# Norms of the query and key blocks: sums of squares as two fp32r products, one unit later

## The chip, the cores and the metric

One core of one Trainium2 chip runs the whole program. The metric is device time of one execution in microseconds; three runs of the kernel before took 979.59, 981.25 and 982.6 us. The profile is of a separate execution.

## The reference

The program is one decoder layer for 1040 prompt rows (16 learned meta tokens and 1024 tokens) and 8 sample rows. Only this part matters here:

```python
z = h @ w_in                                   # 1048 x 3592
qkv, new_buf_qkv = _causal_dwconv(qkv_raw, buf_qkv, conv_qkv_w)   # width 4
qkv = jax.nn.silu(qkv)
q, k, v = jnp.split(qkv, 3, axis=-1)
q = _l2norm(q.reshape(b, length, 4, 128)) * (128 ** -0.5)   # x * rsqrt(sum(x*x) + EPS)
k = _l2norm(k.reshape(b, length, 4, 128))
# then a chunked gated delta rule on q, k, v, an output projection,
# and a mixture of 32 experts of which each row takes 2
```

So each query and key head, a block of 128 channels, is divided by the root of its sum of squares, row by row. In the kernel channels are partitions and rows are columns, so the sum over channels is a sum over partitions. TensorE makes it, as a product of a 128 x 128 matrix of ones with the squares.

## The kernel before, in words

All engines run programs of their own, in a fixed order written out by hand; semaphores hold one back for another. The first half of the program, called the front here, is organised by **units**. The projection has 28 blocks of 128 channels (`NBLK`); each block is made in three units, one for each third of the rows (350 columns), and `UNITS` lists all 84 in order. One unit is 24 matmuls at L1157: eight slices of the inner dimension by three products of high and low parts in fp32r, a format that TensorE multiplies faster than plain fp32 and with fewer bits. `ENDS` gives, for a unit k, the block whose last third it is. Blocks 0 and 1 are interleaved: block 0 ends with unit 3, block 1 with unit 5, block 2 with unit 8, and from there each block n ends with unit 3n+2. Blocks 0 to 7 are keys and queries in turn (`QK` = 8; even ones keys), blocks 8 to 11 values, 12 to 15 gates, 16 to 27 the other mixer.

Every engine has a loop over k, and in step k it does what the order puts there. ScalarE's step k starts when unit k's product is complete, since it copies that third out of PSUM. For a query or key block n that ends with unit e the steps before the change are:

- step e, ScalarE: the last third to `raw`, the first tap of the convolution to `acc` (L672), a strip to `hist`, then `high(n+2)`, the high part `wh` of the weights of block n+2 (L633). VectorE: `weight_low(n+2)`, the low part `wl` (L859), then `conv(n)`, three more taps (L901).
- step e+1: tanh on ScalarE into `th` (L780), `silu(n)` on VectorE (L908) into `acc`.
- step e+2: Square of `acc` into `th` on ScalarE (L788).
- step e+3: TensorE, `square_sums(n)` (L1180) after unit e+3: three plain fp32 products of 358 columns into banks 3 to 5. A plain fp32 product appears as two records, so a group is six. ScalarE: Ln (L765) and Exp (L768, L770), the root's reciprocal, into `th`. Each needs another activation table, so two ACT_TABLE_LOADs belong to it.
- step e+4: VectorE, `normalized(n)` (L913), the product of `acc` and `th`. It gives `kn_ok`.
- step e+5: SyncE writes `acc` to DRAM (L552); ScalarE copies the sample columns (L795).

Around these stand the steps for the decay and key matrices of head h. In step 10+6h TensorE makes `key_products(h)` (L1195) after unit 10+6h, which wait for the normalized block 2h and for Ln of block 2h+1. VectorE copies one block of them (`last_keys`) and makes `decay_args(h)` (L925, L927) when the rows `ar` are loaded. In step 11+6h ScalarE takes their exponential (L774), in step 12+6h VectorE makes `lower(h)` (L935 to L940). SyncE, in order: in step 13+6h it stores both (L538, L540); in step 14+6h it waits until the second store has landed (L542) and loads pieces of it as `lp` (L545); in step 15+6h, which is step 9 of the next head, it loads `ar` and `br` of head h+1 (L533, L499). Block weights are loaded in step e (L494).

Two more places are touched. In step 6 VectorE makes `al` and four small tiles `src` from the decay (L1093 to L1099); in step 7 TensorE transposes `src` after unit 7 (L1307). And from step 35 on VectorE makes an elimination in 38 steps (`eliminate`, L959 and L961) that the chunk stage, from unit 51, needs.

Of the kernel before, what the change touches and what calls it, by code (L numbers as in the profile page):

```python
# [5 lines left out]
F32 = mybir.dt.float32  # L6
F32R = mybir.dt.float32r
I32 = mybir.dt.int32
U32 = mybir.dt.uint32
ALU = mybir.AluOpType  # L10
ACT = mybir.ActivationFunctionType
AX = mybir.AxisListType

P = 128
# [7 lines left out]
TILES = 9  # L22
# [4 lines left out]
QK = 2 * H  # L27
QKV = 3 * H
# [53 lines left out]
def later(i):  # L82
# [9 lines left out]
         ("row_act", 27), ("hi_ok", 18), ("wh_ok", 28), ("wab_hi", 1), ("raw_ok", 12), ("tap0_ok", 12),  # L92
         ("ab_copied", 1), ("th_ok", 12), ("col_a", 9), ("sq_ok", 8), ("rk_act", 16), ("rows_copied", 1),
         ("decay_ok", 4), ("xt_ok", 1), ("kd_ok", 9), ("vc_ok", 9), ("uc_ok", 9), ("o_act", 27), ("normed", 9),
         ("lo_ok", 18), ("wl_ok", 28), ("wab_lo", 1), ("scaled", 3), ("conv_ok", 12), ("col_v", 13),
         ("sl_ok", 12), ("kn_ok", 8), ("kk8_ok", 4), ("diff_ok", 4), ("arg_ok", 4), ("at1_ok", 4), ("at2_ok", 4),
# [140 lines left out]
HALF = 358  # L237
# [4 lines left out]
ENDS = {UNITS.index((n, 2)): n for n in range(NBLK)}  # L242


def end_of(n):

    return UNITS.index((n, 2))
# [62 lines left out]
def front_parts(nc, m, s, b, io):  # L310

    ps = b.psum
# [16 lines left out]
    for k in range(3):  # L329
        at = m.at  # L330
# [7 lines left out]
    th = [m.place(f"th{k}", [P, RLEN]) for k in two]  # L338
# [45 lines left out]
    ck, dt, at, er, nb = [], [], [], [], []  # L384
    for p in two:
        if p == 1:
# [14 lines left out]
    hb = [m.place(f"hb{k}", [P, D]) for k in two]  # L401
    junk = m.place("junk", [P, D])
    wbc = m.place("wbc", [P, D])
    wab = m.place("wab", [P, KD, 8])
    wab1 = m.place("wab1", [P, KD, 16], F32R)
    wab2 = m.place("wab2", [P, KD, 16], F32R)
# [5 lines left out]
    turned, hi_ok, lo_ok, wab_hi, wab_lo = s("turned"), s("hi_ok"), s("lo_ok"), s("wab_hi"), s("wab_lo")  # L412
    w_landed, wh_ok, wl_ok = s.pair("w_landed", 3), s("wh_ok"), s("wl_ok")
    z_done, z_free = s("z_done"), s.pair("z_free", 3)
    ab_ok, ab_copied, ab_turned, zeroed, scaled = (s("ab_ok"), s("ab_copied"), s("ab_turned"), s("zeroed"),
                                                   s("scaled"))
    col_v, col_a, cum_ok, rows_ok, rows_copied, rows_out, zero_out = (
        s("col_v"), s("col_a"), s("cum_ok"), s("rows_ok"), s("rows_copied"), s("rows_out"), s("zero_out"))
    raw_ok, kept, tap0_ok, taps, conv_ok, th_ok, sl_ok = (s("raw_ok"), s("kept"), s("tap0_ok"), s("taps"),
                                                          s("conv_ok"), s("th_ok"), s("sl_ok"))  # L420
    sq_ok, ss_ok, kn_ok, smp_ok = s("sq_ok"), s("ss_ok"), s("kn_ok"), s("smp_ok")
# [45 lines left out]
    def sync(sp):  # L467
# [53 lines left out]
        for k in range(len(UNITS)):  # L521
            n = ENDS.get(k)
# [18 lines left out]
            if 0 <= h < H and ph == 5:  # L541
                sp.wait_ge(at_out, 16 * (h + 1))  # L542
                for blk in range(NS):
                    p0, lo = (blk * H + h) * NC, SB * blk
                    sp.dma_start(lp[p0:p0 + NC, :, :], at_d[:, lo:lo + SB, h, lo:lo + SB]).then_inc(lp_in, 16)  # L545
            for n in (ENDS.get(k - 5), ENDS.get(k - 2)):
                if n is not None and n == ENDS.get(k - 5 if n < QK else k - 2) and n < QKV:
                    if n < QK:
                        sp.wait_ge(kn_ok, n + 1)
                    else:  # L550
                        sp.wait_ge(sl_ok, n + 1)
                    sp.dma_start(qkv_d[conv_index(n), :, 0:PROMPT], acc[n % 3][:, 0:PROMPT]  # L552
                                 ).then_inc(qkv_out[n % 3], 16)
            n = ENDS.get(k - 3)
# [36 lines left out]
            if 0 <= p - 1 < NC and ph == 1:  # L591
                c = p - 1
# [32 lines left out]
    def scalar(act):  # L625
# [103 lines left out]
        for k in range(2, len(UNITS)):  # L729
# [27 lines left out]
            if k == 8:  # L757
                act.wait_ge(rows_ok, 1)
                a_(rows_t[:, :, :], ps[0:2 * NC * H, 7, 0:256].rearrange("p (q t) -> p q t", q=2)[:, :, 0:CH],
                   ACT.Copy).then_inc(rows_copied, 1)  # L760
            n = ENDS.get(k - 3)
            if n is not None and n < QK:
                act.wait_ge(ss_ok, n + 1)
                rk = th[n % 2][:, 0:3 * HALF]
# [21 lines left out]
            if n is not None and n < QK:  # L786
                act.wait_ge(sl_ok, n + 1)
                a_(th[n % 2][:, 0:QLEN], acc[n % 3][:, 0:QLEN], ACT.Square).then_inc(sq_ok, 1)  # L788
            n = ENDS.get(k - 5)
            if n is not None and n < QKV:  # L790
                if n < QK:
                    act.wait_ge(kn_ok, n + 1)
                else:
                    act.wait_ge(sl_ok, n + 1)
                a_(b.smp[:, conv_index(n), :], every(acc[n % 3], QS, KQ), ACT.Copy).then_inc(smp_ok, 1)  # L795
# [42 lines left out]
    def vector(dve):  # L838
# [71 lines left out]
        def normalized(n):  # L910
            dve.wait_ge(sl_ok, n + 1)
            dve.wait_ge(rk_ok.sem, rk_ok.at(n + 1))
            tt(acc[n % 3][:, 0:QLEN], acc[n % 3][:, 0:QLEN], th[n % 2][:, 0:QLEN], ALU.mult).then_inc(kn_ok, 1)  # L913

        def last_keys(h):
            dve.wait_ge(kk_ok, h + 1)
            if h >= 1:
                dve.wait_ge(at1_ok, h)
            V.tensor_copy(kk8[:, :], ps[0:CH, 5, 380:380 + CH]).then_inc(kk8_ok, 1)
# [30 lines left out]
        def identity():  # L950
            inv_step(V.memset(xi[:, :, :], 0.0))
            inv_step(V.memset(xi[:, :, :].rearrange("p r j -> p (r j)")[:, 0:SB * SB:SB + 1], 1.0))
# [71 lines left out]
        for k in range(len(UNITS)):  # L1024
# [6 lines left out]
                softplus_decay()  # L1031
            if k == INV0:
                identity()
            n = ENDS.get(k)
            if n is not None and n + 2 < NBLK and n not in ahead:
                weight_low(n + 2)
# [66 lines left out]
                conv(n)  # L1103
            if n is not None and n >= QKV + H and (n - QKV - H) % 3 == 1:
                conv_a((n - QKV - H) // 3)
            n = ENDS.get(k - 4)
            if n is not None and n < QK:
                normalized(n)
            n = ENDS.get(k - 1)
# [19 lines left out]
    def tensor(pe):  # L1129
# [40 lines left out]
            ins.then_inc(ab_ok, 1)  # L1170

        def square_sums(n):
            pe.wait_ge(sq_ok, n + 1)
            pe.wait_ge(ab_copied, 1)
            if n >= 1:
                pe.wait_ge(ln_ok.sem, ln_ok.at(n))
            if n >= 2:
                pe.wait_ge(kk8_ok, n // 2)
            for c in range(3):
                ins = mm(ps[:, 3 + c, 0:HALF], b.ones[:, :], th[n % 2][:, HALF * c:HALF * c + HALF],  # L1180
                         start=True, stop=True)
            ins.then_inc(ss_ok, 1)

        def key_products(h):
# [105 lines left out]
        for k in range(4, len(UNITS)):  # L1290
            unit(k)
            if k == 4:
                pe.wait_ge(ab_copied, 1)
                pe.wait_ge(scaled, 1)
                for t in range(10):
                    lo, n = (t * CH, length(t)) if t < NC else (PROMPT, SAMPLES)
                    ins = tp(ps[0:n, 6, 16 * t:16 * t + 16], ab[:, lo:lo + n], b.ident[0:16, 0:16])
                ins.then_inc(ab_turned, 1)
            if k == 6:
                pe.wait_ge(col_v, G_STEP)  # L1300
                mm(ps[0:CH, 6, 160:196], b.upto[0:CH, 0:CH], g[0:CH, 0:NC, :], start=True, stop=True)
                mm(ps[0:SAMPLES, 6, 196:200], b.ident[0:SAMPLES, 0:SAMPLES], g[0:SAMPLES, NC, :], start=True, stop=True)
                mm(ps[:, 6, 200:236], b.ones[0:CH, :], g[0:CH, 0:NC, :], start=True, stop=True).then_inc(cum_ok, 1)
            if k == 7:
                pe.wait_ge(col_v, SRC_STEP)
                for q in two:
                    ins = tp(ps[0:2 * NC * H, 7, 128 * q:128 * q + CH],  # L1307
                             src[0:CH, 2 * q:2 * q + 2, :, :].rearrange("p k c h -> p (k c h)"), b.ident[0:CH, 0:CH])
                ins.then_inc(rows_ok, 1)
            n = ENDS.get(k - 3)  # L1310
            if n is not None and n < QK:
                square_sums(n)
            h, ph = (k - 10) // 6, (k - 10) % 6
            if 0 <= h < H and ph == 0:
                key_products(h)
            p, ph = phase(k)
            if 0 <= p - 1 < NC:
                (chain_0, chain_1, chain_2)[ph](p - 1)
            if 0 <= p < NC:
                (prepare_0, prepare_1, prepare_2)[ph](p)  # L1320
            if 0 <= p - 2 < NC and (ph == 2 if p - 2 < NC - 1 else ph == 1):
                output(p - 2)
# [1753 lines left out]
```

## Time and profile before

| | |
|---|---|
| median of 3 runs | 981.25 us |
| profiled execution, whole time | 979.38 us |
| its span | 977.6 us |
| granted TensorE clock, mean | 0.994 |
| TensorE matmul busy | 946.4 us, 97% |
| VectorE busy | 698.6 us, 71% |
| ScalarE busy | 491.2 us, 50% |
| GpSimd busy | 191.5 us, 20% |

The span runs from the first to the last recorded instruction; 1.8 us of the profiled execution lie outside it. Busy shares are averages over stages of different kinds. In the timelines of the profile, the first number is the start in us from the start of the span, the second the time covered by the piece, and "x6" the number of records in it. A bracket at the end gives the time for which the engine was idle just before, and what released it. Matmul records overlap: each lasts about 0.32 us in a unit, while the next starts after 0.16.

### The profile page before, as it was taken

The page shows a single profiled execution, that of the slowest core. Times are in us where ns is not written, and L with a number is a line of the kernel's source. Part 1 is how long each engine was busy: PE and PEld are TensorE (multiplying, and loading weights), DVE is VectorE, ACT ScalarE, POOL GpSimd, SP SyncE. Part 2 cuts the span into 40 slices and gives each one's busy share as a digit, 9 for nine tenths or more (in the row PEclk, how much of TensorE's full clock was granted, in tenths as well). Part 3 has the DMA queues.
Part 4 walks back from the last instruction along what each step waited for, and adds up shares of the span by engine and source line. Part 5 has one row for each costly group of instructions (what it writes and reads, how often), then busy time and mean ns, then how long its engine had stood idle before and what let it go on. Part 6 is the DMA issues. An engine that isn't in the chain of part 4 may idle for free.

```text
span 977.6 us, 14810 instructions
## 1 busy us (share of the span) xinstructions
PE 946.4 (97%) x5408; PEld 817.8 (84%) x5408; DVE 698.6 (71%) x1059; ACT 491.2 (50%) x890; POOL 191.5 (20%) x153
## 2 busy tenths in 40 slices
PE   5999999999899999999999998999999999999996
PEld 4889999999899999999888885667777777777762
DVE  7466677789453634546666666769999999999996
ACT  7578778432423222232422313246666666666794
POOL 2000000000000000000030001315555555554414
PEclk9999999999999999999999999999999999999999
DMA  7104775623755664446833235999999999999994
GB/s 253 52 22 136 176 160 134 176 88 128 229 135 151 166 165 116 123 145 185 290 103 124 71 112 199 345 407 415 412 415 409 409 400 415 396 413 411 393 396 161
DMA packets 123499, 230.61 MB, mean 236 GB/s; under 512 B 71528, under 2 KB 84386, under 8 KB 114734
## 3 DMA queue, kind: packets, MB, share of 16 engines
q1 hardware_dynamic: 108102, 202.69, 60.0%
q0 software_dynamic: 15264, 26.92, 7.4%
q8 instruction: 37, 0.61, 0.3%
q14 instruction: 24, 0.20, 0.1%
q10 hardware_dynamic: 72, 0.20, 0.1%
HBM read 205.33 MB, written 53.11 MB: 264 GB/s over the span
## 4 chain that ended last, share of the span: by engine, by line
PE 86%; DVE 8%; ACT 3%; DMA 1%; issue 1%; SPq 0%; POOL 0%; POOLq 0%; ACTq 0%; DVEq 0%
PE psum L1157 26%; PE psum L2421 12%; PE psum L2075 10%; PE psum L2511 8%; PE psum L2425 5%; PE psum L2357 3%; PE psum L2405 3%; DVE xi L961 2%; DVE it L959 2%; PE psum L2478 2%; PE psum L1180 2%; PE psum L2010 1%; PE psum L1262 1%; DVE acc L901 1%; PE psum L1249 1%
## 5 line engine op out<-in xcount | busy, mean ns | idle before, releaser
L1157 PE MATMUL psum<-hh,wh 128*128 128x350 f32 x672 | 222.7, 331 | 0.7 <-ACT acc L690 0.7
L1157 PE MATMUL psum<-hh,wl 128*128 128x350 f32 x672 | 217.2, 323 | 0.0
L1157 PE MATMUL psum<-hl,wh 128*128 128x350 f32 x672 | 216.5, 322 | 0.0
L1157 PEld LDWEIGHTS psum<-hh,wh 128*128 128x128 f32 x672 | 127.1, 189 | 2.2 <-ACT acc L690 1.0
L1157 PEld LDWEIGHTS psum<-hl,wh 128*128 128x128 f32 x672 | 126.9, 189 | 0.9
L1157 PEld LDWEIGHTS psum<-hh,wl 128*128 128x128 f32 x672 | 126.6, 188 | 0.0
L2395 DVE TENSOR_TENSOR wgu_lo<-wgu,wgu_hi 128x1536 fp32r<-128x1536 f32 x60 | 105.4, 1758 | 17.1 <-ACT wgu_hi L2390 17.0
L2390 ACT ACTIVATE wgu_hi<-wgu 128x1536 fp32r<-128x1536 f32 x60 | 89.3, 1489 | 2.1 <-DMA new_ssm_sample<-s_in 2.1
L2421 PE MATMUL psum<-wgu_hi,xgt_hi 128*128 128x512 f32 x180 | 85.6, 475 | 0.0
L1702 POOL IOTA r_iw<- 128x8 f32 x1 | 0.1, 144 | 410.5 <-DMA mixer_rows<-th 410.5
L859 DVE TENSOR_TENSOR wl<-wst,wh 128x1024 fp32r<-128x1024 f32 x28 | 34.3, 1225 | 58.8 <-ACT wh L633 58.7
L2349 POOL DMA_INDIRECT sum_rows<-total,slot_rows x32 | 66.5, 2078 | 23.5 <-issue 22.1
L2421 PE MATMUL psum<-wgu_lo,xgt_hi 128*128 128x512 f32 x180 | 70.8, 393 | 0.0
L2421 PE MATMUL psum<-wgu_hi,xgt_lo 128*128 128x512 f32 x180 | 70.7, 393 | 0.0
L2491 DVE TENSOR_TENSOR wd_lo<-wd,wd_hi 128x2048 fp32r<-128x2048 f32 x30 | 68.8, 2292 | 1.2
L2118 POOL DMA_INDIRECT xg<-h_rows,slot_rows x34 | 63.5, 1869 | 24.3 <-DVE slot_rows L1933 10.3
L2343 POOL DMA_INDIRECT before<-sum_rows,slot_rows x34 | 34.4, 1012 | 149.2 <-DVE total L2524 142.9
L2487 ACT ACTIVATE wd_hi<-wd 128x2048 fp32r<-128x2048 f32 x30 | 57.7, 1923 | 0.0
L2425 PE MATMUL psum<-wgu,xgt_rest 128*128 128x512 f32 x120 | 56.3, 591 | 0.0
L2375 ACT ACTIVATE xgt_hi<-psum 128x768 fp32r<-128x768 f32 x30 | 24.4, 813 | 61.6 <-PE psum L2357 61.6
L901 DVE SCALAR_TENSOR_TENSOR acc<-raw,cqw,acc 128x1072 f32<-128x1072 f32 x36 | 48.0, 1334 | 0.9
L2075 PE MATMUL psum<-wo_hi,yt_hi 128*128 128x512 f32 (+1 forms) x144 | 47.8, 413 | 0.0
(376 smaller groups left out, 1887.5 us busy)
## 6 DMA issues: line engine op xcount, KB each, us to landing
wgu<-w_gate SPq DMA_DIRECT2D x34, 1024.0 KB
wgu<-w_up SPq DMA_DIRECT2D x34, 1024.0 KB
wd<-w_down SPq DMA_DIRECT2D x34, 1024.0 KB, 13.6
wst<-w_in SPq DMA_DIRECT2D x28, 512.0 KB, 4.2
ck<-qkv_rows SPq DMA_DIRECT2D x9, 702.0 KB
qkv_rows<-acc SPq DMA_DIRECT2D x12, 520.0 KB, 6.4
xb<-x SPq DMA_DIRECT2D x8, 512.0 KB, 4.3
wo<-w_out SPq DMA_DIRECT2D x8, 512.0 KB, 7.1
```

Of the source, the lines that this page charges most:

```text
L901: stt(ac[:, 0:QLEN], rw[:, q:q + QLEN], w[:, q:q + 1], ac[:, 0:QLEN], ALU.mult, ALU.add).then_inc(taps if q < KQ - 1 else conv_ok, 1)
L1157: ins = mm(ps[:, c, 0:ZC], w[:, kk, :], a[:, kk, c * ZC:(c + 1) * ZC], start=(kk == 0 and q == 0), stop=(kk == KD - 1 and q == 2))
L2075: ins = mm(ps[0:n, 2 * (t % 2) + c, :], y, w[:, c * 512:c * 512 + 512], start=(i == 0 and q == 0), stop=(i == KD - 1 and q == 2))
L2118: pool.indirect_dma_start(b.xg[k][:, :], None, b.h2_dram, bass.IndirectOffsetOnAxis(ap=b.slot_rows[:, e:e + 1].bitcast(U32), axis=0), boun ...
L2349: pool.indirect_dma_start(b.sum_d, rows_of(e), rows[:, :], None, bounds_check=TOK - 1, oob_is_err=False).then_inc(q.sum_out.sem, 16)
L2390: nc.scalar.activation(w_hi[x.p][h][:, :, :, :], half_of(b.slots[x.k][0], h), ACT.Copy).then_inc(w_hi_ok[h][x.p].sem, 1)
L2395: nc.vector.tensor_tensor(half_of(b.slots[x.k][1], h), half_of(b.slots[x.k][0], h), w_hi[x.p][h][:, :, :, :].bitcast(F32), ALU.subtract).t ...
L2421: ins = nc.tensor.matmul(gate_up_bank(x.p), a[:, kk, :], w, start=(kk == 0 and i == 0), stop=(kk == KP - 1 and i == 2))
L2425: nc.tensor.matmul(gate_up_bank(x.p), xt_rest[x.p][:, kk - KP, :], raw[:, :, kk, :], start=False, stop=False)
L2487: nc.scalar.activation(wd_hi[x.p][:, :, :], b.slots[x.k][2][:, :, :], ACT.Copy).then_inc(wd_hi_ok[x.p].sem, 1)
L2491: nc.vector.tensor_tensor(b.slots[x.k][3][:, :, :], b.slots[x.k][2][:, :, :], wd_hi[x.p][:, :, :].bitcast(F32), ALU.subtract).then_inc(wd_ ...
L2511: ins = nc.tensor.matmul(ps[0:C, 4 + 2 * x.p + c, :], h[x.p][:, f, :], w[:, f, c * 512:c * 512 + 512], start=(f == 0 and i == 0), stop=(f ...
```

## The change

The squares are split in two as the weights are: ScalarE rounds `th` to fp32r in a new tile `sq_hi`, VectorE subtracts it and gives `sq_lo`. TensorE then makes six fp32r products in place of three plain ones. Everything behind Square moves by one step: sums, Ln and Exp from e+3 to e+4, `normalized` from e+4 to e+5, the store to DRAM and the copy of sample columns from e+5 to e+6. `square_low` stands ahead of `weight_low` in VectorE's step e+3. Both new tiles have one buffer, so the rounding of block n waits for the sums of block n-1 (`ss_ok`). They lie where the input rows lay in the normalization before the front, so the first waits for that too.

```diff
+    sq_hi = m.place("sq_hi", [P, 3 * HALF], F32R, at=pool_b)
+    sq_lo = m.place("sq_lo", [P, 3 * HALF], F32R, at=pool_b + 4320)
...
 # SyncE
-            for n in (ENDS.get(k - 5), ENDS.get(k - 2)):
-                if n is not None and n == ENDS.get(k - 5 if n < QK else k - 2) and n < QKV:
+            for n in (ENDS.get(k - 6), ENDS.get(k - 2)):
+                if n is not None and n == ENDS.get(k - 6 if n < QK else k - 2) and n < QKV:
...
 # ScalarE
-            n = ENDS.get(k - 3)
+            n = ENDS.get(k - 4)
             if n is not None and n < QK:
                 act.wait_ge(ss_ok, n + 1)
...
                 a_(th[n % 2][:, 0:QLEN], acc[n % 3][:, 0:QLEN], ACT.Square).then_inc(sq_ok, 1)
-            n = ENDS.get(k - 5)
-            if n is not None and n < QKV:
+                act.wait_ge(sq_ok, 3 * n + 1)
+                if n == 0:
+                    act.wait_ge(lo_ok, 2 * TILES)
+                else:
+                    act.wait_ge(ss_ok, n)
+                a_(sq_hi[:, :], th[n % 2][:, 0:3 * HALF], ACT.Copy).then_inc(sq_ok, 1)
+            n = ENDS.get(k - 6) if ENDS.get(k - 6, QK) < QK else ENDS.get(k - 5)
+            if n is not None and n < QKV and (n >= QK or k == end_of(n) + 6):
...
 # VectorE
+        def square_low(n):
+            dve.wait_ge(sq_ok, 3 * n + 2)
+            if n >= 1:
+                dve.wait_ge(ss_ok, n)
+            tt(sq_lo[:, :], th[n % 2][:, 0:3 * HALF], sq_hi[:, :].bitcast(F32), ALU.subtract).then_inc(sq_ok, 1)
...
+            n = ENDS.get(k - 3)
+            if n is not None and n < QK:
+                square_low(n)
             n = ENDS.get(k)
             if n is not None and n + 2 < NBLK and n not in ahead:
                 weight_low(n + 2)
...
-            n = ENDS.get(k - 4)
+            n = ENDS.get(k - 5)
             if n is not None and n < QK:
                 normalized(n)
...
 # TensorE
         def square_sums(n):
-            pe.wait_ge(sq_ok, n + 1)
+            pe.wait_ge(sq_ok, 3 * n + 3)
...
             for c in range(3):
-                ins = mm(ps[:, 3 + c, 0:HALF], b.ones[:, :], th[n % 2][:, HALF * c:HALF * c + HALF],
-                         start=True, stop=True)
+                for q, part in enumerate((sq_hi, sq_lo)):
+                    ins = mm(ps[:, 3 + c, 0:HALF], b.ones[:, :].bitcast(F32R), part[:, HALF * c:HALF * c + HALF],
+                             start=(q == 0), stop=(q == 1))
...
-            n = ENDS.get(k - 3)
+            n = ENDS.get(k - 4)
             if n is not None and n < QK:
                 square_sums(n)
```

## Rows read from the trace of the kernel before

**Rows 1.** The page's chain that ended last: share of the span by engine.

```profile
PE 86%; DVE 8%; ACT 3%; DMA 1%; issue 1%; SPq 0%; POOL 0%; POOLq 0%; ACTq 0%; DVEq 0%
```

**Rows 2.** The chain in order of time: start us, us, engine, tile and line.

```profile
68.67 3.87 PE psum L1157 x24
...
82.03 1.84 PE psum L1195 x18
...
87.74 1.81 PE psum L1180 x6
...
169.55 26.94 PE psum L1157 x168
```

**Rows 3.** Busy time of each engine in one stretch of two blocks (us, busy, count).

```profile
101.09:129.66 28.57, 28.57 (x176) 27.23 (x175) 20.53 (x20) 22.47 (x31) 0.00 (x0) 1.00 0.63 153
```

**Rows 4.** Timeline of PE: steps 6 and 7, and the later wait at L1204.

```profile
62.30 2.08 PE L1180 MATMUL psum<-th,ones 128*128 128x358 f32 x6 [1.09 <-ACT th L788]
...
68.28 0.40 PE L1307 MATMUL psum<-ident,src 117*72 117x117 f32 x2
...
261.01 1.08 PE L1204 MATMUL psum<-inv_d,at 117*117 117x117 f32 x8 [2.00 <-DMA inv_t<-inverse_columns]
```

**Rows 5.** Timeline of DVE, steps 5 to 9.

```profile
63.15 4.08 DVE L901 SCALAR_TENSOR_TENSOR acc<-raw,cqw,acc 128x1072 f32<-128x1072 f32 x3
...
68.03 0.20 DVE L1099 SCALAR_TENSOR_TENSOR src<-beta_col,e_col 128x36 f32<-128x36 f32 x1
...
75.53 1.23 DVE L859 TENSOR_TENSOR wl<-wst,wh 128x1024 fp32r<-128x1024 f32 x1 [4.01 <-ACT wh L633]
76.68 4.07 DVE L901 SCALAR_TENSOR_TENSOR acc<-raw,cqw,acc 128x1072 f32<-128x1072 f32 x3
80.84 1.28 DVE L913 TENSOR_TENSOR acc<-acc,th 128x1072 f32<-128x1072 f32 x1
```

**Rows 6.** Timeline of ACT, steps 6 to 8.

```profile
64.41 1.16 ACT L765 ACTIVATE th<-psum,eps 128x1074 f32<-128x1074 f32 x1 [0.24 <-PE psum L1180]
65.58 1.28 ACT L768 ACT_TABLE_LOAD   x1
66.88 1.10 ACT L768 ACTIVATE th<-th 128x1074 f32<-128x1074 f32 x1
...
72.57 0.45 ACT L658 ACTIVATE raw<-psum 128x340 f32<-128x340 f32 x1 [1.10 <-PE psum L1157]
...
74.46 1.04 ACT L633 ACTIVATE wh<-wst 128x1024 fp32r<-128x1024 f32 x1
```

**Rows 7.** Timeline of SP's queue, steps 13 to 15, and of DVE, step 16.

```profile
101.91 0.32 SPq L540 DMA_DIRECT2D lower_blocks<-at_a  x1
...
107.53 1.37 SPq L545 DMA_DIRECT2D lp<-lower_blocks  x3
108.94 0.39 SPq L533 DMA_DIRECT2D ar<-scale_rows  x1
...
114.86 1.26 DVE L925 TENSOR_TENSOR dt_a<-ar,cum 117x1053 f32<-117x1053 f32 x1 [2.12 <-DMA ar<-scale_rows]
```

**Rows 8.** Tile ar: issue to landing of its four loads.

```profile
DMA to landing us min/median/max: 5.2/5.8/6.1
```

**Rows 9.** Tile br: issue to landing of its four loads.

```profile
DMA to landing us min/median/max: 6.4/7.1/8.6
```

**Rows 10.** Timeline of PE near 610 us.

```profile
604.38 2.90 PE L1518 MATMUL psum<-ident,uu 128*128 128x128 f32 x24
608.83 0.41 PE L2018 MATMUL psum<-r_os,before 128*128 128x32 f32 x2 [1.55 <-DVE r_os L1871]
...
610.81 0.66 PE L2027 MATMUL psum<-r_spread,r_in_slot 128*128 128x64 f32 x4 [1.35 <-DVE r_in_slot L1892]
611.31 5.42 PE L1518 MATMUL psum<-ident,uu 128*128 128x128 f32 x32
```

**Rows 11.** One microsecond of that stretch; the granted clock is third from last.

```profile
612.00:613.00 1.00, 1.00 (x7) 1.00 (x6) 0.01 (x1) 0.00 (x0) 0.09 (x1) 0.50 1.07 451
```

More of the change, by code:

```diff
@@ L92 @@
          ("row_act", 27), ("hi_ok", 18), ("wh_ok", 28), ("wab_hi", 1), ("raw_ok", 12), ("tap0_ok", 12),
-         ("ab_copied", 1), ("th_ok", 12), ("col_a", 9), ("sq_ok", 8), ("rk_act", 16), ("rows_copied", 1),
+         ("ab_copied", 1), ("th_ok", 12), ("col_a", 9), ("sq_ok", 24), ("rk_act", 16), ("rows_copied", 1),
          ("decay_ok", 4), ("xt_ok", 1), ("kd_ok", 9), ("vc_ok", 9), ("uc_ok", 9), ("o_act", 27), ("normed", 9),
```

## The prediction

> **What bounds the kernel now.** I read the chain by engine first: TensorE has 86% of it, VectorE 8% [rows 1]. Then the chain in order of time: from unit 6 to unit 35 it never leaves TensorE, whose units, square sums and key products follow each other without a gap until 196.5 us, where the long piece that starts at 169.55 ends [rows 2]. A unit costs 3.87, a group of square sums 1.81 with the switch to plain fp32 and back, a group of key products 1.84 [rows 2]. From 196.5 us VectorE's elimination sets the pace up to the chunk stage; it starts behind unit 35 in program order, so what is won or lost up to there reaches the end one to one. Two blocks with one group of key products take 28.57 us, in which ScalarE is busy 22.47 and VectorE 20.53 [rows 3]: neither bounds a steady pair, but both are full enough for a moved step to count. The one gap of TensorE near the change is 1.09 us ahead of the first group [rows 4].
>
> **The product.** A matmul of 350 columns costs 3.87 / 24 = 0.161 us in a unit [rows 2]; with 358 columns I take 0.163, so six cost 0.98. The group before costs 1.81. Saved: 0.83 per group, 6.6 over eight. The bounds of the new group are 0.97 (six matmuls of a unit) and 1.81 (bits of the switch kept, nothing won).
>
> **The added work beside it.** The rounding of 1074 columns on ScalarE: 1.04 for 1024 columns [rows 6], so about 1.1. VectorE's subtraction: 1.23 for 1024 [rows 5], of which the next instruction overlaps some 0.1; I take 1.2. Per pair ScalarE comes to 22.47 + 2.2 = 24.7 and VectorE to 20.53 + 2.5 = 23.0, against a shortened 28.57 - 1.66 = 26.9. Throughput holds. What must be followed is the order, at three places.
>
> **Place 1, step 7.** TensorE's transposes of `src` start at 68.28, as the last `src` tile is made (68.03 + 0.20) [rows 4, 5]: they were just not late, because the first group filled TensorE's time. Now that group stands in step 7 behind the transposes, so unit 7 follows directly on step 6's small products, at about 61.2, and ends at 65.2. Meanwhile `square_low(0)` stands in VectorE's step 6 behind three taps (end 67.2) [rows 5] and ahead of `al` and `src`: `src` is ready 1.2 later, at 69.4. TensorE stands idle for 4.2 us. Then transposes 0.39, first group 0.98, and unit 8 begins at 70.85 where it began at 68.67: +2.2, with the 1.09 gap and the 2.08 group of before already set against it.
>
> **Place 2, step 10.** The first key products need `normalized(0)`. It stood in step 7; block 0 ends with unit 3, so it now stands in step 8, behind `conv(2)` on VectorE. The chain, from durations less their overlap: first group done 70.9; Ln 1.18, table 1.30, Exp 1.01 [rows 6]; Square 1.1 and rounding of block 1 1.05; ScalarE is free at 76.5, where unit 8 ends at 74.7. Its step 8 takes from 72.57 to the end of `wh`, 75.4, some 2.9 to 3.0 [rows 6], so `wh` is ready at 79.5. Then `weight_low` 1.15, three taps 4.0, product 1.27 [rows 5]: 86.0. TensorE is there at 74.7 + 3.87 + 0.98 + 3.87 = 83.4 and waits 2.6. Key products 1.84 and unit 11 end at 91.8; before, they ended at 87.74 [rows 2]: +4.0.
>
> **The clock.** After gaps of 1.55 and 1.35 us close together the granted clock was 0.50, that is 1.2 GHz, at 612 [rows 10, 11], and 32 matmuls took 5.42 where 24 had taken 2.90 (0.121 each, so 3.87 for 32): 1.55 dearer [rows 10]. After a single gap of 2.00 us at 261.01, eight matmuls took 1.08, with no sign of that [rows 4]. The 4.2 us of place 1 are longer than either, so I count one fall there. It doubles transposes and first group, 1.1 us, which lies on the chain of place 2; the rest, in unit 8, is covered by ScalarE, free 1.8 later than that unit ends. The 2.6 of place 2 shrinks to about 2.1, like the one without a fall. So +1.1, bounds 0 and 3.1 (a second fall, at place 2, with the 1.55 and some of it uncovered). The Trainium skill, "TensorE: Matmul & The Clock Gate", section "What's actually happening", says that the throttled clock is the default and that activity releases it. By that rule the gap of place 1 is paid for again at 1.2 GHz. The rows at 612 agree.
>
> At the end of unit 11 the new kernel is 4.0 + 1.1 = 5.1 behind.
>
> **From there to the last group.** Six groups save 6 x 0.83 = 5.0. Two couplings take some of it back.
> - *VectorE in step e+5.* In odd blocks `lower` ends about 14.2 after unit e's end (store issued at 101.91, unit 11 ended at 87.74) [rows 2, 7]; now `normalized` (1.2) and the next `square_low` (1.2) follow: 16.6. TensorE wants the low part at 3 x 3.85 + 0.98 + 3.85 = 16.4. Blocks 3, 5 and 7: 0.2 each, 0.5 in all (0 to 1.5).
> - *Place 3, SyncE's queue.* The store of `acc` moves from step 13, ahead of the wait for the lower blocks to land, to step 14, behind it and behind `lp`, ahead of `ar` and `br` of the next head. From the end of unit 14: the lower blocks are issued at 1.7 (before 0.8, since the period is shorter); they land 4.5 later (5.6 before, with two transfers behind, now one; bounds 3.5 and 5.6); `lp` 1.4 [rows 7], the store 0.5; `ar` is issued at 8.1. It now has a 520 KB transfer right ahead, as `br` had: `br` lands after 6.4 to 8.6, median 7.1, `ar` after 5.2 to 6.1 [rows 8, 9]. So it lands at 15.2. `decay_args` 2.56 and the low part 1.2 make 19.0, and TensorE wants that at 0.25 + 14.4 + 3.85 = 18.5. Before, VectorE waited 2.12 for `ar` at 114.86 [rows 7] with no one behind it in a hurry; now `square_low` of blocks 4 and 6 is queued there. 0.5 each, 1.0 in all; bounds 0 (landing at 6.4) and 6 (both at 8.6 and slow stores).
>
> **Sum.** 5.1 - 5.0 + 0.5 + 1.0 = +1.6 us at the end of unit 28, carried through to the end. The memory of the new tiles and the one step less of room in `th` cost nothing: tanh of block n+2 comes well behind `normalized(n)` in the steady part, and in step 9 it waits where place 2 already stands. The late copy of sample columns is 0.2 us on ScalarE as before. Against the profiled execution: 979.38 + 1.6 = 981.0. This execution lies 1.9 below the median 981.25, so for the median I say 981.25 + 1.6, about 982.9.
>
> **Rivals.**
> 1. *The arithmetic alone*: the reordering costs nothing. 6.6 from the groups and 1.4 from the first one's gap (1.09) and dearer record (2.08 against 1.81): -8.0, 973. For it: TensorE is the chain throughout. Against it: VectorE's and ScalarE's steps 6 to 8 are in program order, and `src` is already just in time. With only half of places 1 and 2 it would be -4 to -6. 0.15.
> 2. *The loop through SyncE decides*: lower blocks, landing, `lp`, store, `ar`, `decay_args`, `square_low`, square sums. If `ar` lands over 7.6 us after issue, each further microsecond holds TensorE in two heads, and ScalarE's exponential behind it. At `br`'s slowest landing, with stores of 5.6, it is 3 per head in place of 0.5: +1.6 + 5.0 = +6.6; half of that +4, and this with or without a second fall of the clock. 985 to 988. For it: the transfers of a pair come in one burst and the slack of before is 2.1. Against: `ar` never took over 6.1. 0.25.
> 3. *fp32r with the matrix of ones bitcast runs no faster than plain fp32*: six products of the old 0.6, so 8 x (3.6 - 1.8) = 14 slower. The units at 0.161 speak against it. 0.05.
>
> **How the numbers follow.** My case has 0.55, with its own range -1.0 (no fall of the clock, no coupling: 4.0 - 5.0) to +4. A measurement of this kernel can tell about 0.3%, 2.9 us, from no change. Slower than that: 0.25 and 0.05 of the rivals; the tail of my own case beyond +2.9 is about what rival 2 gives back below it. Faster: 0.15. Same: 0.55. The range of 8 in 10 leaves out rivals 1 and 3: 977 to 987.5.
>
> **What would show it.** In the changed kernel: L1307 starts at about 69.5 with some 4 us idle ahead of it, released by VectorE; matmuls behind it at about twice 0.161 for a few microseconds; L1195 near 86 to 87 with about 2 idle, released by VectorE's product; the six records of the sums covering 1.0 us; unit 11 ending at 91.8 to 92.9; later short waits of the sums for `sq_lo`, the longest behind `ar`; the last key products ending 1 to 2 us later than 169.55. I am wrong if TensorE shows no gap at step 7 or 10 (rival 1), if waits of over 1.5 us stand ahead of the sums of blocks 4 and 6 (rival 2), or if the end of unit 35 and the end of the kernel move by different amounts.

## The result, and the profile after

The changed kernel took 983.95 us in the median of 21 runs, against 981.25 us before; the ratio is 1.0026, 95% interval 1.0015 to 1.0037, so 1.5 to 3.6 us slower. 982.9 was forecast, with a range of 977 to 987.5. The profiled execution took 983.95 us, with a span of 982.1, which is 4.5 us more than that of before; the median moved by 2.7.

The one place to read the change at is the end of unit 35, ahead of the elimination. Executions start with transfers, and what follows them starts up to 1.6 us earlier or later, so I count from the small products of step 6 (`upto`, in both kernels the same work up to there), which start at 60.44 before and 60.65 after. ScalarE's copy of the last third of unit 35, which starts when the unit's product is complete, in ScalarE's timeline before and then after:

```profile
196.51 0.46 ACT L658 ACTIVATE raw<-psum 128x340 f32<-128x340 f32 x1 [1.68 <-PE psum L1157]
...
198.91 0.46 ACT L660 ACTIVATE raw<-psum 128x340 f32<-128x340 f32 x1 [1.68 <-PE psum L1174]
```

That is 136.07 and 138.26 us behind the mark: +2.19. Place 1 in TensorE's timeline after, to be held against [rows 4]; L1174 is the unit, L1198 the sums, L1325 the transposes:

```profile
65.03 0.32 PE L1174 MATMUL psum<-hh,wl 128*128 128x350 f32 x1
69.66 0.61 PE L1325 MATMUL psum<-ident,src 117*72 117x117 f32 x2 [4.30 <-DVE src L1116]
69.94 0.65 PE L1198 MATMUL psum<-sq_hi,ones 128*128 128x358 f32 x1
70.38 0.50 PE L1198 MATMUL psum<-sq_lo,ones 128*128 128x358 f32 x1
70.67 0.50 PE L1198 MATMUL psum<-sq_hi,ones 128*128 128x358 f32 x1
70.97 0.50 PE L1198 MATMUL psum<-sq_lo,ones 128*128 128x358 f32 x1
...
71.87 0.49 PE L1174 MATMUL psum<-hh,wh 128*128 128x350 f32 x1
...
73.08 0.33 PE L1174 MATMUL psum<-hh,wl 128*128 128x350 f32 x1
73.25 0.33 PE L1174 MATMUL psum<-hh,wh 128*128 128x350 f32 x1
```

The bracket shows a gap of 4.30 us and who ended it. From sum to sum it is 0.30 us, against 0.17 from 73.08 to 73.25: that is the low clock. Busy times in the stretch itself (the granted clock, third from last, is 0.50, that is 1.2 GHz):

```profile
69.60:72.70 3.10, 3.04 (x11) 3.03 (x12) 1.28 (x2) 1.32 (x2) 0.00 (x0) 0.50 0.03 5
```

VectorE after, to be held against [rows 5]. The low part L927 sits between the taps and `src`; at 85.78 is `normalized(0)`, behind the taps of block 2:

```profile
63.36 4.08 DVE L909 SCALAR_TENSOR_TENSOR acc<-raw,cqw,acc 128x1072 f32<-128x1072 f32 x3
67.35 1.27 DVE L927 TENSOR_TENSOR sq_lo<-th,sq_hi 128x1074 fp32r<-128x1074 f32 x1
...
69.41 0.20 DVE L1116 SCALAR_TENSOR_TENSOR src<-beta_col,e_col 128x36 f32<-128x36 f32 x1
...
81.79 4.07 DVE L909 SCALAR_TENSOR_TENSOR acc<-raw,cqw,acc 128x1072 f32<-128x1072 f32 x3
85.78 1.27 DVE L921 TENSOR_TENSOR acc<-acc,th 128x1072 f32<-128x1072 f32 x1
```

Place 2, and then the groups of blocks 3 and 4, in TensorE's timeline after:

```profile
87.10 2.10 PE L1213 MATMUL psum<-acc 128*117 128x117 f32 x18 [2.11 <-DVE acc L921]
...
109.74 0.43 PE L1198 MATMUL psum<-sq_hi,ones 128*128 128x358 f32 x1 [0.32 <-DVE sq_lo L927]
110.01 0.33 PE L1198 MATMUL psum<-sq_lo,ones 128*128 128x358 f32 x1
110.17 0.32 PE L1198 MATMUL psum<-sq_hi,ones 128*128 128x358 f32 x1
...
124.93 0.43 PE L1198 MATMUL psum<-sq_hi,ones 128*128 128x358 f32 x1 [0.55 <-DVE sq_lo L927]
```

From the last matmul of a unit to the first of the next, less the 0.16 that it takes anyway, a group before costs 1.53, and the switch back to fp32r 0.28 more behind it: the 1.81 of [rows 2]. After, the groups of blocks 2 to 7 cost 0.99, 1.57, 1.80, 1.01, 1.19 and 1.35. 0.99 is the bare product; the other 1.97 us are waits for the low part. Such a wait costs some 0.25 more than the idle time in its bracket (0.58 for the 0.32 of block 3): 0.16 because that idle time is counted from the end of a record, while the next one otherwise starts 0.16 ahead of it, and the rest because the first step behind it is longer (109.74 to 110.01 is 0.27, the next step 0.16). For block 4 the wait comes through SyncE's queue and VectorE, to be held against [rows 7, 8]:

```profile
107.33 0.32 SPq L542 DMA_DIRECT2D lower_blocks<-at_a  x1
...
112.58 1.15 SPq L547 DMA_DIRECT2D lp<-lower_blocks  x3
113.77 0.38 SPq L554 DMA_DIRECT2D qkv_rows<-acc  x1
114.20 1.53 SPq L535 DMA_DIRECT2D ar<-scale_rows  x1
```

```profile
121.14 1.26 DVE L939 TENSOR_TENSOR dt_a<-ar,cum 117x1053 f32<-117x1053 f32 x1 [2.15 <-DMA ar<-scale_rows]
122.43 1.26 DVE L941 TENSOR_TENSOR dt_a<-dt_a,negmask 117x1053 f32<-117x1053 f32 x1
123.61 1.27 DVE L927 TENSOR_TENSOR sq_lo<-th,sq_hi 128x1074 fp32r<-128x1074 f32 x1
```

The account: unit 11 ends 5.13 us later than before, the six groups win 6 x 1.81 - 7.91 = 2.95, which leaves 2.18. The page's chain of the execution after looks quite different from [rows 1]:

```profile
PE 74%; DVE 9%; DMA 7%; ACT 4%; issue 3%; POOL 1%; SPq 1%; POOLq 0%; ACTq 0%; DVEq 0%
```

Some 113 us have left TensorE in it. Cut into stretches, the chain is on TensorE for 134 of the 150 us from 50 to 200 before and for 66 after: at each small wait it goes over to VectorE, ScalarE or a transfer and stays there for a while, so these shares say little of what a wait costs. Another 30 us left between 600 and 650 us and 14 behind 930, in stages that the change does not touch. Nor do these stages take the same time in each execution: from the experts' product L2425 (L2443 after) at 650.20 and 652.25 to the first record of TensorE's last product, L2305 (L2323 after), it is 316.7 us before and 318.9 after, and in the experiments 317.7 to 321.4, in no order of the change. These 2.2 us are the other half of the 4.5 between the two spans. So the spans of single executions are not compared below, only the end of unit 35 and the ratios of many runs.

### The profile page after: what moved, and what is told of

It is laid out like the page before. It is cut to its first block, busy times and chain, and to the rows that moved or that the text cites. A ratio compares the mean times of both kernels' runs of the same rounds, so it can differ in the third digit from the quotient of the medians.

```text
span 982.1 us, 14840 instructions
## 1 busy us (share of the span) xinstructions
PE 944.6 (96%) x5408; PEld 820.0 (83%) x5408; DVE 707.0 (72%) x1067; ACT 499.2 (51%) x898; POOL 191.2 (19%) x153
## 4 chain that ended last, share of the span: by engine, by line
PE 74%; DVE 9%; DMA 7%; ACT 4%; issue 3%; POOL 1%; SPq 1%; POOLq 0%; ACTq 0%; DVEq 0%
PE psum L1174 20%; PE psum L2439 13%; PE psum L2093 11%; PE psum L2529 8%; PE psum L2443 5%; PE psum L2375 3%; DMA new_ssm_sample<-s_in 2%; DVE xi L975 2%; DVE it L973 2%; DVE acc L909 1%; PE psum L2028 1%; DMA y<-sum_rows 1%; DVE wl L867 1%; PE psum L1280 1%; PE psum L1267 1%
## 5 line engine op out<-in xcount | busy, mean ns | idle before, releaser
L1174 PE MATMUL psum<-hh,wh 128*128 128x350 f32 x672 | 220.9, 329 | 0.7 <-ACT acc L692 0.7
L1174 PE MATMUL psum<-hh,wl 128*128 128x350 f32 x672 | 217.5, 324 | 0.0
L1174 PE MATMUL psum<-hl,wh 128*128 128x350 f32 x672 | 216.7, 322 | 0.0
L1174 PEld LDWEIGHTS psum<-hh,wh 128*128 128x128 f32 x672 | 127.4, 190 | 1.3 <-ACT acc L692 0.9
L1174 PEld LDWEIGHTS psum<-hl,wh 128*128 128x128 f32 x672 | 127.1, 189 | 0.0
L1174 PEld LDWEIGHTS psum<-hh,wl 128*128 128x128 f32 x672 | 126.8, 189 | 0.0
L2443 PE MATMUL psum<-wgu,xgt_rest 128*128 128x512 f32 x120 | 56.3, 591 | 0.0
```

Source lines behind the costliest of these rows:

```text
L1174: ins = mm(ps[:, c, 0:ZC], w[:, kk, :], a[:, kk, c * ZC:(c + 1) * ZC], start=(kk == 0 and q == 0), stop=(kk == KD - 1 and q == 2))
L2443: nc.tensor.matmul(gate_up_bank(x.p), xt_rest[x.p][:, kk - KP, :], raw[:, :, kk, :], start=False, stop=False)
```

## The experiments

Each was executed twelve times, e8 six times. Ratios are to the kernel before, executed beside them; most intervals are 2 to 4 us to either side, so for steps of a microsecond the end of unit 35, counted from step 6's small products, decides.

| kernel | ratio, 95% interval | end of unit 35, us | against before |
|---|---|---|---|
| before | 1 | 136.07 | |
| changed | 1.0026, 1.0015 to 1.0037 | 138.26 | +2.19 |
| e1 product alone | 0.9967, 0.9939 to 0.9996 | 131.83 | -4.24 |
| e2 order alone | 1.0059, 1.0034 to 1.0083 | 142.64 | +6.57 |
| e3 filled gap | 1.0043, 1.0000 to 1.0086 | 137.05 | +0.98 |
| e4 first norm | 1.0012, 0.9974 to 1.0050 | 135.95 | -0.12 |
| e5 src first | 1.0014, 0.9995 to 1.0034 | 138.16 | +2.09 |
| e6 store back | 1.0013, 0.9983 to 1.0043 | 138.57 | +2.50 |
| e7 first two old | 0.9976, 0.9952 to 0.9999 | 133.10 | -2.97 |
| e8 high only | 0.9923, 0.9894 to 0.9953 | 129.74 | -6.33 |
| e9 early ar | 1.0010, 0.9986 to 1.0033 | 138.06 | +1.99 |
| e10 both | 0.9971, 0.9945 to 0.9996 | 132.79 | -3.28 |
| e11 low before norm | 0.9944, 0.9911 to 0.9978 | 131.10 | -4.97 |

### The product and the order apart

```diff
 # e1, on the kernel before
-                a_(th[n % 2][:, 0:QLEN], acc[n % 3][:, 0:QLEN], ACT.Square).then_inc(sq_ok, 1)
+                a_(sq_hi[:, 0:QLEN], acc[n % 3][:, 0:QLEN], ACT.Square).then_inc(sq_ok, 1)
...
+                for q in range(2):
+                    ins = mm(ps[:, 3 + c, 0:HALF], b.ones[:, :].bitcast(F32R), sq_hi[:, HALF * c:HALF * c + HALF],
+                             start=True, stop=True)
```

> The order of the kernel before, every step where it was; Square writes its result straight into an fp32r tile, and each of the three products is made twice from it as fp32r, so that TensorE has the six matmuls of the change and nothing else is added. Left out: the low part of the squares. Theory (the product saves 0.83 us a group, the moved order takes it back at the start): 8 x 0.83 and the 1.4 us at the first group, 8.0 us faster than before; of that 1.09 may stay, since the first group still waits for Square: 6.9 to 8.0 faster, about 974. Rival (the product itself saves little in place, since ScalarE and VectorE set the pace of a pair of blocks): within 2 us of before.

Measured: 3.2 us faster by the ratio, 4.24 at unit 35; neither the 7 to 8 of the theory nor the rival's 2 at most. Four of its groups cost 0.98 and three 1.44; those three wait for Square:

```profile
100.91 1.25 PE L1187 MATMUL psum<-sq_hi,ones 128*128 128x358 f32 x6 [0.19 <-ACT sq_hi L794]
```

Its first group still waits for Square and then the transposes for `src` (0.8). So in the old place the sums are bound to ScalarE as soon as a pair of blocks gets shorter, and the gain of the product alone is about half of 8.0. The move by one unit does answer something.

```diff
 # e2, on the changed kernel
-                for q, part in enumerate((sq_hi, sq_lo)):
-                    ins = mm(ps[:, 3 + c, 0:HALF], b.ones[:, :].bitcast(F32R), part[:, HALF * c:HALF * c + HALF],
-                             start=(q == 0), stop=(q == 1))
+                ins = mm(ps[:, 3 + c, 0:HALF], b.ones[:, :], th[n % 2][:, HALF * c:HALF * c + HALF],
+                         start=True, stop=True)
```

> The changed kernel with its order, its rounding and its subtraction, but the three plain fp32 products of th as before. Theory: it has the gaps of steps 7 and 10, the fall of the clock, and a first group dearer by some 1.2 us at the low clock; after unit 11 no gain and no loss: 6 to 7 us slower than before, 4 us slower than the changed kernel. Rival (the added work costs wherever it stands, some 0.6 us a pair of blocks, and the start only 1 or 2): 3 to 4 us slower than before, spread evenly over blocks 0 to 7.

Measured: +5.8 us by the ratio, +6.57 at unit 35, near the theory's 6 to 7. Its two gaps are 4.31 and 1.67, its groups from block 2 on cost 1.53 or 1.54 each, without a wait, and a pair of blocks takes 28.55 as before: all of the loss lies ahead of unit 11. The rival, a price spread evenly, is out.

### The start: clock, first product, src

```diff
 # e3, on the changed kernel
             if k == 7:
+                for q in range(24):
+                    mm(ps[:, 7, 0:ZC], wh[0][:, q % KD, :], hh[:, q % KD, 0:ZC], start=True, stop=True)
                 pe.wait_ge(col_v, SRC_STEP)
```

> The changed kernel with 24 extra fp32r matmuls of 350 columns behind unit 7, ahead of the wait for src, into a bank that is written anew right after: 3.9 us of work in the 4.3 us gap. Theory (the gap lets the clock fall to 1.2 GHz, and what this costs the first group and the transposes lies on the chain to the key products): the matmuls behind the gap are at 0.16 us from start to start, unit 11 ends 1.1 us earlier than in the changed kernel, and the whole is 1.1 faster than that, +1.4 against before. Rival (the slow matmuls are hidden by the wait of step 10 anyway): no change against the changed kernel, +2.5 against before.

The extra matmuls are L1324; the gap shrinks to 0.48, and the same stretch as above runs at full clock:

```profile
70.83 0.39 PE L1327 MATMUL psum<-ident,src 117*72 117x117 f32 x2 [0.48 <-DVE src L1116]
70.98 0.41 PE L1198 MATMUL psum<-sq_hi,ones 128*128 128x358 f32 x1
71.24 0.33 PE L1198 MATMUL psum<-sq_lo,ones 128*128 128x358 f32 x1
71.40 0.33 PE L1198 MATMUL psum<-sq_hi,ones 128*128 128x358 f32 x1
```

```profile
69.60:72.70 3.10, 2.62 (x17) 2.33 (x16) 2.31 (x7) 2.32 (x5) 0.00 (x0) 1.00 0.00 0
```

The unit behind the first key products starts 27.32 behind the mark, against 28.32 in the changed kernel: 1.00 of the forecast 1.1. Unit 35 ends 1.21 earlier. In the ratio, whose interval is 8 us wide (1.0000 to 1.0086), that can't be seen.

```diff
 # e4, on the changed kernel
-            n = ENDS.get(k - 5)
-            if n is not None and n < QK:
+            n = 0 if k == 7 else ENDS.get(k - 5)
+            if n is not None and n < QK and (n > 0 or k == 7):
                 normalized(n)
```

> The changed kernel with normalized(0) in VectorE's step 7 instead of step 8, ahead of the three taps of block 2. Theory (the first key products wait for it alone): the 2.1 us gap ahead of them is gone, and the whole is 2.1 faster than the changed kernel, +0.4 against before, within 0.4. Rival (Ln of block 1, or the rows that ScalarE copies in step 8, come as late): a gap of 1 to 2 us stays ahead of the key products with another releaser, and less than 1 us is won.

TensorE goes on without a gap, where the changed kernel waits 2.11:

```profile
85.21 0.32 PE L1174 MATMUL psum<-hh,wl 128*128 128x350 f32 x1
85.37 0.88 PE L1213 MATMUL psum<-acc 128*117 128x117 f32 x7
```

Unit 35 ends 2.31 earlier than in the changed kernel, 0.12 earlier than before. One instruction of VectorE, one step earlier, takes the whole loss of the change back at unit 35; the ratio, 0.9974 to 1.0050, can't tell it from either kernel.

```diff
 # e5, on the changed kernel: square_low(0) no longer ahead of weight_low in step 6, but here
                 assert cols == SRC_STEP
+                square_low(0)
```

> The changed kernel with square_low(0) behind the src tiles in VectorE's step 6 instead of ahead of them. Theory (what TensorE stands for in step 7 is VectorE's order, taps first, and both the transposes and the first group hang on it): the gap ahead of the transposes shrinks by 1.2 us to 3.1, but the first group now waits some 0.5 for the low part, so it starts only 0.3 to 0.5 earlier; unit 35 ends 0.3 to 0.6 earlier than in the changed kernel. Rival (the transposes alone hold it): 1.2 us earlier.

```profile
69.20 0.39 PE L1326 MATMUL psum<-ident,src 117*72 117x117 f32 x2 [3.13 <-DVE src L1116]
```

3.13 of gap as expected, then 0.92 for the low part, where some 0.5 was expected: the unit behind the key products starts 0.47 earlier (27.85 against 28.32), as the theory said. But only 0.10 is left at unit 35, since the group of block 4 costs 2.13 instead of 1.80. What is won ahead is taken by that wait: first sign that the later waits are a chain of their own.

### The later waits

```diff
 # e6, on the changed kernel
-            for n in (ENDS.get(k - 6), ENDS.get(k - 2)):
-                if n is not None and n == ENDS.get(k - 6 if n < QK else k - 2) and n < QKV:
+            for n in (ENDS.get(k - 5), ENDS.get(k - 2)):
+                if n is not None and n == ENDS.get(k - 5 if n < QK else k - 2) and n < QKV:
```

> The changed kernel with SyncE's store of a query or key block back in step e+5, ahead of lp, ar and br. Theory (the groups of blocks 4 and 6 wait for ar through decay_args and the low part): ar is issued about when it is now but lands about 1 us sooner, as before; TensorE's interval at the group of block 4 falls from 1.80 to 1.0 to 1.2 us, that of block 3 (1.57, which hangs on lower) stays; unit 35 ends 0.6 to 1.0 earlier. Rival (VectorE's added instructions make these waits, not the transfers): nothing moves.

The group of block 4 fell to 1.15, as expected, and still unit 35 ended 0.31 later. SyncE's first store now stands ahead of `ar` of head 0 and waits for the late `normalized(0)`:

```profile
86.91 0.33 SPq L554 DMA_DIRECT2D qkv_rows<-acc  x1
87.28 0.43 SPq L535 DMA_DIRECT2D ar<-scale_rows  x1
```

so VectorE waits 2.60 for `ar` and the group of block 2 costs 1.67; and block 6 now costs 1.97. My expectation missed that the store stands on both sides of an `ar`.

```diff
 # e7, in short: blocks 2 to 7 as in the changed kernel, 0 and 1 as before, the store as in e6
+def stage(k, d):          # n < 2: step e+d; 2 <= n < QK: step e+d+1
...
         def square_sums(n):
+                if n < 2:
+                    ins = mm(ps[:, 3 + c, 0:HALF], b.ones[:, :], th[n % 2][:, HALF * c:HALF * c + HALF],
+                             start=True, stop=True)
+                    continue
```

> Blocks 0 and 1 keep the plain fp32 product and the order of the kernel before; blocks 2 to 7 have the changed product, a unit later; SyncE's store in step e+5. Theory (the loss is all in steps 6 to 10, and the six later groups gain 0.83 each but for waits): no gap at steps 7 and 10, no fall of the clock, unit 11 ends as before; the six groups give 5.0 less 0.5 to 1.5 of waits: unit 35 ends 3.5 to 4.5 earlier than before, and the whole is as much faster, 0.996 of before. Rival (the later blocks lose what they gain to the fuller ScalarE and VectorE once the start no longer lags): within 1.5 us of before.

No gap at steps 7 and 10, unit 11 ends as before, and unit 35 ends 2.97 earlier; 3.5 to 4.5 was too much. The six groups cost 1.00, 1.47, 1.63, 1.00, 1.84 and 0.98: waits of 1.98 us. The longest:

```profile
148.12 0.43 PE L1213 MATMUL psum<-sq_hi,ones 128*128 128x358 f32 x1 [0.59 <-DVE sq_lo L938]
```

```diff
 # e8, on the kernel before: as e1, each product once
```

> As the first experiment, with each product made once: three fp32r matmuls of the high part in the order of the kernel before. Left out: the low part of the squares. Theory (in the old place the sums wait for Square, which the full ScalarE brings late as soon as a pair of blocks gets shorter): of the 0.49 us that each group is cheaper than in the first experiment no more than a third is won, unit 35 ends 4.2 to 5.5 earlier than before. Rival (TensorE's own work is the bound): 8 x 0.49 more, 8 us earlier than before.

Unit 35 ends 2.1 earlier than in e1, about half of the 3.9 by which the groups' own work got cheaper: between the theory, at most a third of it, and the rival, all of it. Blocks 1, 2, 4 and 6 cost 0.48 and keep all of it; blocks 3, 5 and 7 cost 1.48, and the first group still waits:

```profile
100.35 0.77 PE L1187 MATMUL psum<-sq_hi,ones 128*128 128x358 f32 x3 [0.72 <-ACT sq_hi L794]
```

```diff
 # e9, on the changed kernel
-                if h >= 1:
-                    sp.wait_ge(diff_ok, h)
-                sp.dma_start(ar[:, :, :], rows_d[0, :, h, :].partition_broadcast(P)).then_inc(ar_in, 16)
+                if h == 0:
+                    sp.dma_start(ar[:, :, :], rows_d[0, :, h, :].partition_broadcast(P)).then_inc(ar_in, 16)
                 beta_rows(h)
+            if 0 <= h < H - 1 and ph == 3:
+                sp.wait_ge(diff_ok, h + 1)
+                sp.dma_start(ar[:, :, :], rows_d[0, :, h + 1, :].partition_broadcast(P)).then_inc(ar_in, 16)
```

> The changed kernel with the rows ar of the next head loaded in SyncE's step 12+6h, as soon as decay_args has read the last ones, and so ahead of the stores and of lp; nothing else moved. Theory (the groups of blocks 4 and 6 wait for ar through decay_args and the low part, and moving the store back only moved the waits, since the loop over lower, landing, lp and ar stayed): VectorE no longer waits for ar, TensorE's interval at the group of block 4 falls from 1.80 to about 1.0, unit 35 ends 0.6 to 1.2 earlier than in the changed kernel. Rival (ScalarE, with 24.7 us of work in a pair and two waits of 1 us for silu, is as long a loop by itself, near 27 us): block 4 gets its 0.8 back and others lose it, unit 35 within 0.3.

VectorE doesn't wait for `ar` at all and the groups of blocks 4 and 6 cost 0.99. But blocks 3, 5 and 7 cost 1.58 each, and unit 35 gains 0.20: the rival's number. Its reason is another matter. VectorE in step 17 to 20 of this kernel:

```profile
130.53 1.28 DVE L918 SCALAR_TENSOR_TENSOR acc<-th,acc 128x1072 f32<-128x1072 f32 x1 [2.08 <-ACT th L784]
131.72 1.19 DVE L951 SCALAR_TENSOR_TENSOR at_a<-psum,dt_a 117x468 f32<-117x468 f32 x2
...
133.14 1.26 DVE L956 TENSOR_TENSOR at_a<-at_a,br 117x1053 f32<-117x1053 f32 x1
134.31 1.27 DVE L923 TENSOR_TENSOR acc<-acc,th 128x1072 f32<-128x1072 f32 x1
135.50 1.27 DVE L929 TENSOR_TENSOR sq_lo<-th,sq_hi 128x1074 fp32r<-128x1074 f32 x1
```

silu, `lower`, `normalized`, low part, back to back, and TensorE waits for the last. This execution also shows what covers the clock: the granted clock was still 0.50 from 71.50 to 75.00, where the changed kernel's came back near 72.7, and units 8 and 9 took 1.3 us longer than there (71.44 to 80.70 against 71.87 to 79.82). Still the unit behind the key products starts at 28.32 behind the mark in both, since the gap ahead of them was 0.81 instead of 2.11.

> Blocks 0 and 1 as in the kernel before, the others changed, and ar loaded in step 12+6h; the store of blocks 2 to 7 in step e+6 as in the changed kernel. The waits of the low part that are left here are the price of the fuller VectorE and ScalarE. Theory: unit 35 ends 3.3 to 4.5 earlier than before (the same without early ar: 2.97), the whole 0.995 to 0.997 of before. Rival (the loop is ScalarE's): 2.7 to 3.2 earlier, as without it.

(The edits of e7 and e9 together, the store in step e+6.) 3.28 earlier at unit 35, short of the theory's 3.3 to 4.5. Blocks 3, 5 and 7 cost 1.47, 1.57 and 1.57, the others 0.99.

```diff
 # e11, on e10, in short: for the odd n of 2 to 7; the even ones stay ahead of weight_low
-            n = ENDS.get(k - 3)        # ahead of weight_low
+            n = ENDS.get(k - 2)        # ahead of normalized
+            if n is not None and 2 <= n < QK and n % 2 == 1:
+                square_low(n)
             n = stage(k, 4)
             if n is not None:
                 normalized(n)
```

> The kernel of the tenth experiment (blocks 0 and 1 as before, ar loaded early), with square_low of the odd blocks 3, 5 and 7 one step earlier on VectorE, ahead of normalized of the block before instead of behind it. Theory (what is left of the waits is VectorE's order in odd blocks: lower, normalized, low part, one behind the other): TensorE's interval at their groups falls from 1.47 to 1.57 to 1.0, a pair of blocks from 27.5 to 26.9, unit 35 ends 4.5 to 5.0 us earlier than before (3.28 in the tenth), the whole near 0.995 of before. Rival (ScalarE's loop of about 27.5 a pair): the waits come back in the next group or ahead of the key products, unit 35 within 0.3 of the tenth.

```profile
100.38 1.26 DVE L967 TENSOR_TENSOR at_a<-at_a,br 117x1053 f32<-117x1053 f32 x1
101.55 1.27 DVE L940 TENSOR_TENSOR sq_lo<-th,sq_hi 128x1074 fp32r<-128x1074 f32 x1
102.73 1.27 DVE L935 TENSOR_TENSOR acc<-acc,th 128x1072 f32<-128x1072 f32 x1
```

All six groups cost 0.99 or 1.00, a pair of blocks takes 26.9, and unit 35 ends 4.97 earlier, which is 6 x 0.83. The ratio is 0.9944, 0.9911 to 0.9978: 5.5 us faster than before (2.2 to 8.7), a version that beats both kernels. ScalarE's loop is not the bound.

## Why the prediction was right

Its number was 1.6 us slower, at unit 35 it is 2.19, over all runs 2.55.

- *The product.* 0.98 per group and 0.83 saved were forecast; it is 0.99 and 0.82 wherever nothing waits. e11 shows the six groups' 5.0 in full.
- *Place 1.* 4.2 us of gap forecast, 4.30 measured, released by `src`, from 69.6 instead of 69.4. e5 shows the low part's share: with it out of the way the gap is 3.13. The rest is the group of sums that no longer fills it: with the group back in its old place (e7) the gap is gone.
- *Place 2.* With the low clock: key products at 86.0 + 1.1 = 87.1 with a gap of 2.1; measured 87.10 with 2.11, and 0.2 of that is the later start of the execution. The links came as computed: the first group done at 71.9 (70.9 + 1.1 forecast), `wh` ready at 80.6 (79.5 + 1.1), and `normalized(0)` ending at 87.05. e4 shows that this gap is worth 2.3.
- *The clock.* It fell, to 0.50 for 3.1 us, behind the 4.30 gap and not behind the 2.11 one. The forecast took a gap of 2 us to be harmless from one row, the wait of 2.00 at 261.01 [rows 4]; that was partly luck. Behind the same wait, 1.89 to 1.95 us long, the clock fell to 0.50 in five of the eleven experiments (e1, e2, e6, e9, e10), which cost 1.5 to 1.6 us each time; in the other executions, among them one of 1.87 and that of 2.00, it did not. At place 2 it fell in none of six executions with gaps of 0.81 to 2.51. e3 puts 1.0 on it at place 2, against the forecast 1.1; that the rest is covered is seen in e9.
- *Up to unit 11.* 5.1 forecast, 5.13 measured. e2, with the old product in the new order, has its whole loss there.
- *The later waits.* Here the size was off: 0.5 and 1.0 forecast, 1.5 in all, and 1.97 measured. For odd blocks I had 0.2 each, from 16.6 against 16.4; the groups of 3, 5 and 7 lost 0.58, 0.02 and 0.36, together 0.96. For blocks 4 and 6 I had 0.5 each, they lost 0.81 and 0.20: the sum of 1.0 is met, the parts are not. Two things were missing. A wait costs some 0.25 beside its idle time, and in the changed kernel the idle times of these groups, 0.32, 0.55 and 0.10, are only half of the 1.97. And the two kinds are links of one loop, in which what one group waits the next need not: e5, e6 and e9 each took one wait away and had it back elsewhere, within 0.3 us at unit 35. Only when both links were cut, `ar` in e9's way and VectorE's order in e11's, did they go (with blocks 0 and 1 in the old order; with the changed start it was not tried).
- *Carried through to the end.* The elimination's last step came at 246.81 before and 249.18 after, 2.16 more from the mark, and it starts 50.3 us behind ScalarE's copy in all thirteen profiled executions: up to there the loss is carried one to one. The first product of the chunk stage was only 1.8 later than before, as a wait for transfers in between varies by itself. The ratio's interval, 1.5 to 3.6 us, holds the 2.19. The spans of the two profiled executions moved by 4.5 instead, which was named as a sign of being wrong; the rest of it lies behind 936 us and has no part in the change that a run shows. That the stages in between give nothing back or take nothing on average is not shown more finely than by the ratio.

Of the rivals, the third fell with the first sums at full clock, 0.16 us from one to the next. The arithmetic alone fell too: the product in the old order (e1) wins only 4.2, as the sums then wait for Square, and half of the forecast 8.0 is not to be had even there, where the low part and its work are left out. The loop through SyncE existed, and cost 0.81 and 0.20 rather than 3 per head; `ar` landed in 6.92 us ahead of block 4 and in 5.95 ahead of block 6, where I had 7.1.

## What to carry to other kernels

When a helper is moved behind another step, walk the two or three first rounds by themselves: an irregular start (here two interleaved blocks) can turn one step of delay into a wait behind four microseconds of someone else's work, though the steady part has room. Where a wait is removed and comes back in the neighbouring round, look for the loop and cut all its links at once. And a faster product may be worth half in the old order (e1) and less than nothing in a new one (the change), and all of it, in the groups that have it, when the order is made for it (e11).

## What was not expected of the hardware

The clock of TensorE also fell in places that the change does not touch. In the profiled execution after it was at 0.50 from 490 to 494 us, where it was 1.00 before, among small products and with no gap of TensorE in it:

```profile
490.00:494.00 4.00, 4.00 (x14) 3.50 (x14) 3.44 (x20) 1.54 (x5) 0.00 (x0) 0.50 0.01 4
```

and at 612 to 620 us it was the other way round, 0.81 before and 0.99 after. The lag of the execution after was 2.0 us before the first place, 5.2 behind it, and 2.05 at 650. In e11 the same place also cost 3.2 us, in the other eleven executions 0.4 at most. With the falls behind the wait at 261 us, single executions of nearly the same work differ by some 1.5 us in one place and 3 us in another, and a change of 2 us is not to be read there.
